# Two-layer hybrid diffusion step: the steady conditioning products move from TensorE to VectorE, TensorE only turns the sums

## The reference

```python
def adaln_params(cond, w_ada_l, b_ada_l):
    mod = jax.nn.silu(cond) @ w_ada_l + b_ada_l
    return jnp.split(mod, 3, axis=-1)
...
shift, scale, gate = adaln_params(c_ctx, w_ada[l], b_ada[l])
h = rms_norm(xp, norm_gain[l]) * (1.0 + scale) + shift
z = h @ p["w_in"]
...
term = gates[..., i * D_MODEL:(i + 1) * D_MODEL] * (y @ p["w_branch"][i])
out = merged @ p["w_out"]
xp = xp + gate * out
```

## Time and profile before

| | |
|---|---|
| Median of 3 runs | 1451.22 us (1450.38 to 1451.79) |
| The profiled execution: its time | 1451.13 us |
| its span, first to last instruction | 1449.3 us |
| mean granted TensorE clock | 0.995 of 2.4 GHz |
| PE busy | 1381.8 us |
| DVE busy | 781.8 us |
| ACT busy | 571.3 us |
| POOL busy | 78.8 us |

### The profile page before, as it was taken

How to read it: one execution, slowest core, us unless ns; L and a number is a source line. 1 busy time by engine, 2 the same in 40 slices (tenths; PEclk the granted TensorE clock), 3 DMA queues, 4 the chain that set the end, 5 groups by cost and what they waited for, 6 DMA issues and landing times.

```text
span 1449.3 us, 27315 instructions
## 1 busy us (share of the span) xinstructions
PE 1381.8 (95%) x10581; PEld 1324.7 (91%) x10581; DVE 781.8 (54%) x1646; ACT 571.3 (39%) x1249; POOL 78.8 (5%) x102
## 2 busy tenths in 40 slices
PE   4899999999999999999999999999999999999998
PEld 1799889999989999999999988999998999999998
DVE  2556676556554256443564576763755524654355
ACT  2456555324443222222344555542345422222242
POOL 2000000010000000000010000001100000001000
PEclk9999999999999999999999999999999999999999
DMA  9411122023002342355332121212220134214321
GB/s 324 141 59 63 46 65 65 32 74 109 31 30 92 125 135 66 125 152 173 98 117 78 63 66 37 73 55 76 76 66 31 33 117 142 73 38 117 117 74 73
DMA packets 114501, 127.73 MB, mean 88 GB/s; under 512 B 4076, under 2 KB 109128, under 8 KB 114376
## 3 DMA queue, kind: packets, MB, share of 16 engines
q1 hardware_dynamic: 108344, 109.77, 23.8%
q0 software_dynamic: 4624, 15.22, 3.5%
q10 hardware_dynamic: 1408, 0.99, 0.2%
HBM read 119.66 MB, written 6.31 MB: 87 GB/s over the span
## 4 chain that ended last, share of the span: by engine, by line
PE 79%; DVE 10%; ACT 4%; issue 4%; DMA 1%; POOL 1%; SPq 0%; DVEq 0%; ACTq 0%; POOLq 0%
PE G L1345 37%; PE G L1343 19%; PE BK L1359 8%; PE TO L1426 3%; PE TP L1413 3%; PE BK L1370 2%; PE TP L1389 2%; PE S L1404 1%; DVE w_lo L1032 1%; DMA merged<-in_w_ada 1%; DVE neg_max L1168 1%; POOL rs L705 1%; ACT w_hi L837 1%; PE S L1407 1%; PE S L1406 1%
## 5 line engine op out<-in xcount | busy, mean ns | idle before, releaser
L1032 DVE TENSOR_TENSOR w_lo<-w_raw,w_hi 128x512 fp32r<-128x512 f32 x312 | 207.6, 687 | 127.2 <-ACT w_hi L837 126.0
L1345 PE MATMUL G<-h_lo,w_hi 128*128 128x320 f32 x1472 | 249.7, 312 | 0.0
L1345 PE MATMUL G<-h_hi,w_hi 128*128 128x320 f32 x1472 | 248.1, 311 | 0.0
L1345 PE MATMUL G<-h_hi,w_lo 128*128 128x320 f32 x1472 | 247.8, 310 | 0.0
L1345 PEld LDWEIGHTS G<-h_lo,w_hi 128*128 128x128 f32 x1472 | 222.6, 188 | 3.4 <-issue 2.9
L1345 PEld LDWEIGHTS G<-h_hi,w_hi 128*128 128x128 f32 x1472 | 222.0, 188 | 0.8 <-issue 0.3
L1345 PEld LDWEIGHTS G<-h_hi,w_lo 128*128 128x128 f32 x1472 | 222.4, 188 | 0.2
L837 ACT ACTIVATE w_hi<-w_raw 128x512 fp32r<-128x512 f32 x312 | 185.3, 624 | 35.0 <-DMA w_raw<-in_w_in 23.1
L909 ACT ACTIVATE tg<-G 128x320 f32<-128x320 f32 x128 | 55.8, 436 | 249.9 <-PE G L1345 248.6
L1343 PE MATMUL G<-w_hi,h_hi 128*128 128x256 f32 x960 | 138.1, 287 | 5.8 <-ACT w_hi L837 3.3
L945 ACT ACTIVATE work<-S,neg_max 128x640 f32<-128x640 f32 (+1 forms) x120 | 85.3, 712 | 143.9 <-DVE neg_max L1168 129.6
(11 more groups left out here) (214 smaller groups left out, 1540.8 us busy)
## 6 DMA issues: line engine op xcount, KB each, us to landing
w_raw<-in_w_mgate SPq DMA_DIRECT2D x32, 1024.0 KB, 5.6
w_raw<-in_w_in SPq DMA_DIRECT2D x30, 1024.0 KB, 5.4
w_raw<-in_w_ada SPq DMA_DIRECT2D x20, 1024.0 KB, 5.7
w_raw<-in_w_branch SPq DMA_DIRECT2D x32, 256.0 KB, 6.0
w_raw<-in_w_out SPq DMA_DIRECT2D x8, 1024.0 KB, 5.3
merged<-in_w_ada SPq DMA_DIRECT2D x4, 1024.0 KB, 13.5
work<-in_x_sample POOLq DMA_DIRECT2D x4, 512.0 KB, 5.9
work<-gate_rows POOLq DMA_DIRECT2D x4, 512.0 KB, 4.1
```

The costliest lines, as they stand in the source:

```text
L1032: V.tensor_tensor(w_lo[:, s.n % 2, a:b, :], raw_rows(s), w_hi[:, s.n % 2, a:b, :].bitcast(F32), ALU.subtract).then_inc(lo_done, 1)
L1345: ins = mm(g[:, 0:HALF], a[:, w, kt, c], b[:, kt, half], start=first, stop=last)
```

## The change

The 16 steady quarters become 8 blocks of 512 columns, each loaded in two halves of 512 rows (`kh`), still 1 MB a load and one with each of the same 16 chunks. `ada` and `adat` remain for the eight early quarters alone. For each half come four `adav` steps, after passes 5 to 8 (3 + i behind `delay`): DVE multiplies 128 rows of the block, 128x512, by the conditioning value of each row, once for each of the two vectors, and adds into `ada_sum`. The very first multiplication of a block writes it and adds nothing. So 128 DVE operations in all, each pair waiting for the one before. After the second half, in the following chunk (after passes 10 and 11), come two `adas` steps: four transposes each turn a vector's 512 sums into a half of S, and DVE sums these over 128 elements and adds the bias. `ada_sum` lies over the part of `k_stack` that attention B doesn't use. S was used by `map` and `rscore` alone; these now wait for `as_evac` too. SP loads the next block when `ada_added` says that the last pair is done. `gate_out` and `scales` wait for `as_evac`.

```diff
--- before.py
+++ after.py
@@ -156,7 +156,7 @@
         return [Step("split", l=c.l, n=c.n, part=i, of=c) for i in range(4 if c.branch is None else 5)]
 
     early = [Step("asplit", l=0, c=c, q=1) for c in range(8)]
-    later = [(0, c) for c in range(8, 12)] + [(1, c) for c in range(12)]
+    later = [(l, g, kh) for l, g in ((0, 4), (0, 5), (1, 0), (1, 1), (1, 2), (1, 3), (1, 4), (1, 5)) for kh in range(2)]
     for l in range(DEPTH):
 
         phases = []
@@ -299,10 +299,11 @@
             _, c, delay, gap = e
 
             if later and (c.branch in (1, 2) or (c.src == "w_in" and C_Q <= c.col < D_Q)):
-                l, a = later.pop(0)
-                load = Step("asplit", l=l, c=a)
-                due += [(passes + delay + 1, load), (passes + delay + 5, Step("ada", l=l, c=a, of=load)),
-                        (passes + delay + 7, Step("adat", l=l, c=a))]
+                l, a, kh = later.pop(0)
+                load = Step("asplit", l=l, c=a, half=kh)
+                due.append((passes + delay + 1, load))
+                due += [(passes + delay + 3 + i, Step("adav", l=l, c=a, half=kh, part=i, of=load)) for i in range(4)]
+                due += [(passes + delay + 8 + i, Step("adas", l=l, c=a, half=i)) for i in range(2 * kh)]
             if c.n in nxt:
                 due.append((passes + delay, nxt[c.n]))
                 due += [(passes + delay + gap * i, p) for i, p in enumerate(pieces(nxt[c.n]))]
@@ -319,7 +320,7 @@
 def number(plan):
 
     n = dict.fromkeys(("big", "big_act", "out", "bk", "tg", "tp", "hturn", "to", "sc", "maps", "exps", "rscore",
-                       "adat", "pieces", "raw", "pow", "es", "head", "comb", "cat", "hstat", "ysplit", "msplit", "mod",
+                       "adat", "adav", "adas", "pieces", "raw", "pow", "es", "head", "comb", "cat", "hstat", "ysplit", "msplit", "mod",
                        "qturn", "kdecay", "qdecay", "ada", "asplit", "vec", "bkd"), 0)
     raw_total = [0] * EARLY
     chunk_used = {}
@@ -345,6 +346,12 @@
             n["pieces"] += 1
             s.of.last_piece = s.piece = n["pieces"]
             pieces_of[s.n] = n["pieces"]
+        if k == "adav":
+            n["adav"] += 2
+            s.of.last_use = n["adav"]
+        if k == "adas":
+            n["adas"] += 1
+            s.sc_exp, s.sc_sm = n["exps"], n["rscore"]
         if k == "ada":
             s.a = n["ada"]
             n["ada"] += 1
@@ -500,7 +507,9 @@
         merged = sb("merged", [P, KT, TOK])
         za = sb("za", [P, NT, 512])
         zv = sb("zv", [P, NT + 1, 256])
+        k_at = nc.sbuf_base
         k_stack = sb("k_stack", [P, 8, 6 * P], F32R)
+        ada_sum = nc.alloc_sbuf_tensor_at("ada_sum", [P, 2, 512], F32, offset=k_at + 4 * 6 * P * 4)
         q_stack = sb("q_stack", [P, 2, 4, P], F32R)
         work = sb("work", [P, 4 * TOK + 2 * TOK + 1024])
         y_hi = sb("y_hi", [P, 2, TOK], F32R)
@@ -553,6 +562,9 @@
 
             return w_raw[:, i, 0:KT, :] if i < RAW else mflat[:, KT * CW * (i - RAW):KT * CW * (i - RAW + 1)].rearrange("p (k n) -> p k n", k=KT)
 
+        def ada_half(s):
+            return raw_slot(s.slot).rearrange("p (a b) n -> p a (b n)", b=2)
+
         def raw_rows(s):
             a, b = s.rows
             return raw_slot(s.of.slot)[:, a:b, :] if b <= KT else w_raw[:, s.of.slot, a:b, :]
@@ -585,7 +597,8 @@
         raw_in = [sem(f"raw_in{i}") for i in range(EARLY)]
         small_in = sem("small_in")
         tables_in, cols_ready, tanh_done, cond_ready = sem("tables_in"), sem("cols_ready"), sem("tanh_done"), sem("cond_ready")
-        ada_used = sem("ada_used")
+        ada_used, ada_added = sem("ada_used"), sem("ada_added")
+        as_done, as_evac = sem("as_done"), sem("as_evac")
         mask_exp, mask_done = sem("mask_exp"), sem("mask_done")
         params_in, consts_in, cache_in = sem("params_in"), sem("consts_in"), sem("cache_in")
         x_in, xr_in = [sem(f"x_in{t}") for t in range(NT)], sem("xr_in")
@@ -649,8 +662,14 @@
                 if s.kind in ("load", "asplit"):
                     if s.last and s.last.kind == "load":
                         sp.wait_ge(lo_done, s.last.last_piece)
+                    elif s.last and s.last.q == 1:
+                        sp.wait_ge(ada_used, s.last.a + 1)
                     elif s.last:
-                        sp.wait_ge(ada_used, s.last.a + 1)
+                        sp.wait_ge(ada_added, s.last.last_use)
+                    if s.kind == "asplit" and s.q == 0:
+                        sp.dma_start(ada_half(s), t_in["w_ada"][s.l][4 * P * s.half:4 * P * (s.half + 1), 512 * s.c:512 * s.c + 512]
+                                     .rearrange("(k p) c -> p k c", p=P)).then_inc(raw_in[s.slot], 16)
+                        continue
                     sp.dma_start(raw_slot(s.slot), raw_chunk(s)).then_inc(raw_in[s.slot], 16)
                     if s.kind == "load" and s.branch is not None:
                         q = (s.col % DM)
@@ -718,6 +737,7 @@
                         pool.dma_start(t_out["state"][0, s.l, d].rearrange("h k v -> k h v"), ctx_state[64 * d:64 * d + 64, :, :]).then_inc(cache_out, 16)
                 if s.kind == "gate_out":
                     pool.wait_ge(to_evac, s.before["to"])
+                    pool.wait_ge(as_evac, s.before["adas"])
                     pool.wait_ge(tp_evac, s.before["tp"])
                     pool.wait_ge(cache_out, 16 * 6 * (s.l + 1))
                     for c in range(2):
@@ -1040,11 +1060,33 @@
                     m = mod[:, s.l, 2 * s.c:2 * s.c + 2, :]
                     after(V.tensor_reduce(m, TO[:, 0:2 * P].rearrange("p (b j r) -> p b r j", b=2, j=4)[:, :, 0:2, :], AX.X, ALU.add))
                     V.tensor_tensor(m, m, cols[:, b0:b0 + 2].unsqueeze(2).broadcast_to([P, 2, 2]), ALU.add).then_inc(to_evac, 1)
+                elif k == "adav":
+                    dve.wait_ge(raw_in[s.of.slot], s.of.raw_target)
+                    if s.half == 0 and s.part == 0:
+                        dve.wait_ge(as_done, s.before["adas"])
+                        dve.wait_ge(sc_done, s.before["sc"])
+                    elif s.before["adav"]:
+                        dve.wait_ge(ada_added, s.before["adav"])
+                    row = ada_half(s.of)[:, s.part, :]
+                    for c in range(2):
+                        w = cond[:, 4 * s.half + s.part, c:c + 1]
+                        if s.half == 0 and s.part == 0:
+                            V.tensor_scalar(ada_sum[:, c, :], row, w, None, ALU.mult).then_inc(ada_added, 1)
+                        else:
+                            V.scalar_tensor_tensor(out=ada_sum[:, c, :], in0=row, scalar=w, in1=ada_sum[:, c, :],
+                                                   op0=ALU.mult, op1=ALU.add).then_inc(ada_added, 1)
+                elif k == "adas":
+                    dve.wait_ge(as_done, s.before["adas"] + 1)
+                    b0 = R_BADA + 24 * s.l + 4 * s.c
+                    m = mod[:, s.l, 4 * s.c:4 * s.c + 4, s.half:s.half + 1]
+                    after(V.tensor_reduce(m, S[:, 512 * s.half:512 * s.half + 512].rearrange("p (b n) -> p b n", b=4), AX.X, ALU.add))
+                    V.tensor_tensor(m, m, cols[:, b0:b0 + 4].unsqueeze(2), ALU.add).then_inc(as_evac, 1)
                 elif k == "scales":
                     dve.wait_ge(to_evac, s.before["to"])
                     if s.l == 0:
                         dve.wait_ge(ada_used, s.before["ada"])
                     if s.l > 0:
+                        dve.wait_ge(as_evac, s.before["adas"])
                         dve.wait_ge(hh_done, NT * s.l)
                     V.scalar_tensor_tensor(out=gs[:, :, :], in0=mod[:, s.l, KT:2 * KT, :], scalar=1.0,
                                            in1=cols[:, R_GAIN + KT * s.l:R_GAIN + KT * (s.l + 1)].unsqueeze(2).broadcast_to([P, KT, 2]),
@@ -1376,6 +1418,17 @@
                     for b in range(2):
                         ins = nc.tensor.transpose(TO[:, b * P:(b + 1) * P], ada_rows[:, b * P:(b + 1) * P], ident)
                     ins.then_inc(to_done, 1)
+                elif k == "adas":
+                    if s.sc_exp:
+                        pe.wait_ge(exp_done, s.sc_exp)
+                    if s.sc_sm:
+                        pe.wait_ge(sm_done, s.sc_sm)
+                    if s.before["adas"] >= 2:
+                        pe.wait_ge(as_evac, s.before["adas"] - 1)
+                    pe.wait_ge(ada_added, s.before["adav"])
+                    for b in range(4):
+                        ins = nc.tensor.transpose(S[:, 512 * s.half + b * P:512 * s.half + (b + 1) * P], ada_sum[:, s.half, b * P:(b + 1) * P], ident)
+                    ins.then_inc(as_done, 1)
                 elif k == "hturn":
                     tp_free(s)
                     pe.wait_ge(xs_done, s.l * NT + s.t + 1)
@@ -1393,6 +1446,8 @@
                         pe.wait_ge(exp_done, s.sc_exp)
                     if s.sc_sm:
                         pe.wait_ge(sm_done, s.sc_sm)
```

(2 more changed lines are left out.)

## The result

| | before | after |
|---|---|---|
| median, 4 runs each | 1450.80 us (1448.85 to 1451.79) | 1437.16 us (1435.77 to 1438.49) |
| profiled execution: time | 1451.13 us | 1438.49 us |
| its span | 1449.3 us | 1436.6 us |

What follows compares the result with a forecast made beforehand. PE was taken to bound the kernel, busy 95% of the span with 79% of the chain. -22.6 + 7.0 + 1.6 + 0.3 + 1.8 = -11.9 us from 1451.2 gave 1439.3 us, range 1435.0 to 1446.0.

Steps and rivals of the forecast that it cites:

- What is taken from PE: Sixteen steady conditioning steps leave PE, `ada` 1.19 and `adat` 0.22 us each by the chain: 22.6 us removed.
- the turns: 16 `adas` steps of four transposes added on PE, 0.44 us each: 7.0 us added.
- Net -15.6: PE's balance in us: 22.6 removed by the steady steps, 7.0 added by the new turns.
- Hidden on DVE: DVE's added pairs, 1.45 us each, and reductions fit beside PE's work, costing nothing except at three places.
- (a): Turn into the fourth gate group, 612 to 620 us: pairs delay L1225 by 0.45, PE's 1.19 saving lost; +1.6 us.
- (b): Turn right ahead of yturn and `rscore`: score product waits for S, +0.8, L1471's 0.5 wait goes; +0.3 us.
- (c): End of the last gate chunk, 687 to 703 us: DVE's pairs and reduction delay L1281, PE waits; +1.8 us.
- 1, all hidden: Reductions and pairs on DVE cost nothing even at the gate-group turn and last gate chunk's end; 1435.6 us, chance 0.20.
- 2, DVE behind in the retention stretch: Five norms and three loads there each stall PE about 0.7 us, 5.6 us more; 1444.9 us, chance 0.16.
- 3, late landing: Raw w_ada buffer arrives late in eight gate chunks, DVE waits, 22.4 us more; 1461.7 us, chance 0.06.
- 10.3 us of cover: Time from a w_ada load's issue until DVE wants it in gate chunks; landings longer than this cost time.

Runs made afterwards that it cites:

- E1: Changed kernel with every DVE multiply-and-add after a block's first pair working on 1 column instead of 512; span 1431.9 us.
- E2: Changed kernel with the pairs on 1 column for only two of 16 loads, second halves of blocks 1 and 3 of layer 1; span 1434.2 us.
- E7: Changed kernel with every pair one pass earlier; 1434.42 us, ratio 0.9892 to the kernel before.
- E4: Changed kernel with each pair but a block's first done twice, about 78 us more on DVE; 1497.96 us.
- E9: Changed kernel with the four transposes of each steady turn done twice; 1442.05 us.
- E3: Changed kernel with both turns of a block after the same pass; span 1434.7 us.
- E5: Changed kernel with each half block loaded by two transfers of 256 columns, so rows of 1 KB instead of 2 KB; 1434.49 us.
- E6: Changed kernel with loads of each gate group's last chunk moved to the output projection's first two chunks, and a block's turns together; 1433.54 us, ratio 0.9884.
- E8: Changed kernel with every pair one pass earlier and both turns of layer 1's first block after the same pass; 1433.02 us, ratio 0.9882.
- E10: Kernel before the change with four of the eight matmuls of each steady product; 1440.55 us, against 1449.20 before.
- E11: Changed kernel run again unaltered, for its spread; 1436.67 us, ratio 0.991.

## Why the prediction was right

**What is taken from PE.** Right to 1%: -22.5 measured, -22.6 forecast, and the turns 0.43 against 0.44. It was the gaps and lengthened passes along the chain that gave these prices. The matmuls' own mean of the earlier trace rows, 379 ns, times 8 would have given 3 us for a step that cost 1.20. Net -15.6 stands.

**Hidden on DVE.** Right as far as was tried: in E1 the pairs of 14 of the 16 loads give nothing back when they are shortened. The pair took 1.46 (four operations in 2.92 us, next fence) against 1.45. DVE's busy total came to 863.4 us, where I had 872.

**(a).** DVE's operations at the turn into the fourth gate group answer to the earlier trace rows:

```profile
607.13 0.43 DVE L1258 TENSOR_TENSOR o_s<-o_s,rs 128x256 f32<-128x256 f32 x1 [1.19 <-POOL rs L733]
607.48 2.92 DVE L1076 SCALAR_TENSOR_TENSOR ada_sum<-w_raw,cond_w,ada_sum 128x512 f32<-128x512 f32 x4
610.32 0.48 DVE L1142 SCALAR_TENSOR_TENSOR tg<-tg,BK 128x320 f32<-128x320 f32 x1
...
611.24 0.42 DVE L1267 TENSOR_TENSOR gy<-TO,gy 128x256 f32<-128x256 f32 x1
613.00 1.49 DVE L1168 TENSOR_TENSOR y_lo<-gy,y_hi 128x1280 fp32r<-128x1280 f32 x1 [1.34 <-ACT y_hi L983]
```

From the norm result (607.13) to L1267 (611.24) it is 4.11 us, where it was 3.84 (612.81 to 616.65): +0.27, where I had +0.45, beside the 1.20 that PE could not use. 1.5 in place of 1.6.

**(b).** PE's turn, the transposes of y and the score product:

```profile
567.41 0.60 PE L1430 MATMUL S<-cst,ada_sum 128*128 128x128 f32 x4
567.85 0.38 PE L1493 MATMUL TO<-cst,o_s 128*128 128x128 f32 x2
569.19 0.72 PE L1520 MATMUL S<-work 64*128 64x128 f32 x8 [0.96 <-DVE mod L1083]
```

The wait is 0.96 us (0.8 forecast); the wait at L1471 that it replaces gave back 0.75 (0.5 forecast). Net 0.3 as forecast, by two errors that cancel.

**(c), the step whose size was off.** "So the 1.41 - 0.88 = 0.5 us that PE saves there is lost, and 1.3 more: +1.8." DVE's operations there, which answer to the earlier trace rows:

```profile
679.21 0.49 DVE L1146 TENSOR_TENSOR merged<-merged,tg 128x320 f32<-128x320 f32 x1
679.62 1.41 DVE L1076 SCALAR_TENSOR_TENSOR ada_sum<-w_raw,cond_w,ada_sum 128x512 f32<-128x512 f32 x2
680.95 1.22 DVE L1314 TENSOR_TENSOR h_lo<-merged,h_hi 128x1024 fp32r<-128x1024 f32 x1
682.08 1.41 DVE L1076 SCALAR_TENSOR_TENSOR ada_sum<-w_raw,cond_w,ada_sum 128x512 f32<-128x512 f32 x2
683.41 1.22 DVE L1314 TENSOR_TENSOR h_lo<-merged,h_hi 128x1024 fp32r<-128x1024 f32 x1
684.55 0.48 DVE L1142 SCALAR_TENSOR_TENSOR tg<-tg,BK 128x320 f32<-128x320 f32 x1
...
686.68 3.50 DVE L1314 TENSOR_TENSOR h_lo<-merged,h_hi 128x1024 fp32r<-128x1024 f32 x3 [1.12 <-ACT h_hi L988]
690.09 0.68 DVE L1082 TENSOR_REDUCE mod<-S 128x4 f32<-128x512 f32 x1
...
691.49 0.42 DVE L1323 TENSOR_TENSOR ra<-G,work 128x256 f32<-128x256 f32 x1
```

DVE is done with BK's second result at 679.21 + 0.49 = 679.70, and L1323 starts at 691.49, 11.79 us later; before, 699.05 - 688.03 = 11.02. That is +0.77, where I had +1.25, and this 0.5 is what the sum came out too high: PE's wait at the bank grew from 0.98 us (the 1.18 of the earlier trace rows is that of its weight load) to 2.29, by 1.3 and not by 1.8 (E1 and E2 gave back 1.2 of it). I added pairs of 1.45 and msplits of 1.2, whole durations with a wait. In the trace the next operation starts before the last one ends: a pair and msplit are 1.33 and 1.13 apart (679.62, 680.95, 682.08). Five such seams of 0.08 us from 679.62 to 684.55, and the 0.04 of waiting that I had put into each of the two pairs, make up the 0.5. It is the overlap that the earlier trace rows shows between two like operations, here between operations of different kind too.

I had weighed it against a rule of the Trainium skill ("VectorE: DVE Perf Modes", "The DRAIN you can't avoid"), by which the next operation does not start until the pipe is empty. The same section goes on that an operation that isn't held starts earlier, which I left out. The trace agrees with that second sentence: its operations do start earlier, by 0.08 us at these seams. So the section did not speak against the 1.45.

**Rivals.** 1, all hidden: no, E1 finds 2.6 us, though with the pairs early (E7) it comes true at (a) and (c). 2, DVE behind in the retention stretch: no, not a unit there but (a) changed in E1; E4 shows that twice the work would have brought it. 3, late landing: no. The landings of SP's 16 loads of `w_ada` (L670):

```profile
DMA to landing us min/median/max: 5.0/5.2/7.6
```

The longest is 7.6 us, of 10.3 us of cover, and no operation of DVE waits for these loads. Before, the longest of all loads in these stretches was 10.6. E7, with a pass less of cover, loses nothing.

## What to carry to other kernels

Price a step on the bounding engine by the chain around it, with and without the step, and not by the durations of its instructions. Here, work moved to an engine that was half idle was free except at the few turns where that engine itself hands over the next stage; look these up in the order of instructions, and keep the moved work one place away from them. The room for it was the distance to whoever reads its result and to whoever waits for its buffer (E4), which a busy share in a window doesn't show.

## What was not expected of the hardware

**PE's clock falls in one execution and not in the next, after the same wait.** At the turn of the layers PE waits for w_hi. Before, its next two passes:

```profile
764.48 1.94 PE L1343 MATMUL G<-w_hi,h_hi 128*128 128x256 f32 x8 [2.32 <-ACT w_hi L837]
766.23 1.91 PE L1343 MATMUL G<-w_hi,h_lo 128*128 128x256 f32 x8
```

and after:

```profile
756.93 1.19 PE L1385 MATMUL G<-w_hi,h_hi 128*128 128x256 f32 x8 [2.33 <-ACT w_hi L857]
757.96 1.12 PE L1385 MATMUL G<-w_hi,h_lo 128*128 128x256 f32 x8
```

Waits of 2.32 and 2.33 us; yet the first passes then start 1.75 us apart, the others 1.03. The windows of before show the granted clock there (the number behind POOL's):

```profile
760.00:765.00 5.00, 2.68 (x22) 2.50 (x21) 3.79 (x9) 4.44 (x10) 1.40 (x2) 0.96 0.18 74
765.00:770.00 5.00, 5.00 (x33) 5.00 (x33) 1.58 (x3) 0.39 (x1) 0.60 (x2) 0.70 0.80 263
```

0.70 of 2.4 GHz as a mean of 5 us, so part of it at the lower level, 1.2 GHz. It costs 1.5 us. From the 136th unit's start to the 156th's it is 67.0 us in before, E1, E2 and E9, which have this step, and 65.5 in the changed kernel, E3, E5, E6, E7, E8, E10 and E11, which don't (in E6 once its two added turns of 0.43 are taken off); E4, whose clock fell in many places, is left out. Nothing in their edits goes with it. (E3 lost 1.28 us in the same way at another place, behind a wait of 3.10 us.) A step of 1.3 us stands in the opening too: from unit 2 to unit 16 it is 52.0 or 52.1 us in before, the changed kernel, E2, E6 and E8, and 50.8 in E1, E3, E5, E7, E9, E10 and E11. The window that holds it, in the changed kernel and then in E3:

```profile
97.00:110.00 13.00, 10.89 (x68) 10.66 (x67) 8.62 (x22) 7.73 (x22) 0.00 (x0) 0.87 0.24 81
```

```profile
97.00:110.00 13.00, 10.79 (x77) 10.32 (x76) 9.33 (x24) 9.18 (x23) 0.00 (x0) 1.00 0.25 81
```

The granted clock is 0.87 in the one and 1.00 in the other. Executions of one kernel spread over 3.3 us (1434.87 to 1438.14 in E11), though the stretches under study repeat to 0.12 us between its two profiles. That steps like these make up most of the spread is likely but not shown, as only one execution of each run has a profile. It is why a term of 1 us is read from the units' starts here and not from the medians. What decides whether the clock falls was not tried.
